# A two-layer mixer kernel: the change of layers overlapped with the last products, and q's and k's rotary products, a tanh and a weight sum moved in time

## The chip, the cores and the metric

The kernel is one program on one core of a Trainium2 chip, written for the engines directly: TensorE (PE, matrix products), VectorE (DVE), ScalarE (ACT), GpSimd (POOL) and SyncE (SP, which here only issues DMAs). Each engine runs its own list of instructions in order; they meet at semaphores. The metric is the device time of one execution in microseconds, the median of several.

## The reference

Each of two layers normalises x (1024 rows of 1024), projects it with one large matrix, runs four token mixers on slices of the projection, gates them, projects again and adds to x. A last norm follows.

```python
for l in range(DEPTH):                     # DEPTH = 2
    h = _rmsnorm(x, norm_g[l])
    p = h @ w_in[l]
    ...                                    # split into pa, pb, pc, pd, dz, pg
    oa = _chunk_band_attention(...) * silu(az)
    ob = _hgrn2(...) * silu(bz)
    oc = _dsa(_rope(q), _rope(k), v, _rope(qi), _rope(ki), cwi) * silu(cz)
    od = _rwkv7(...) * silu(dz)
    y = sum(sigmoid(g) * (o @ w_branch[l, n]))   # over the four mixers
    x = x + y @ w_out[l]
return _rmsnorm(x, final_g)
```

In `_dsa` each query keeps its 256 keys of largest index score.

## The kernel before, in words

All is in float32. The transposed normalised input `hT` (8 tiles of 128 features x 1024 rows) stays in SBUF. The large projections are done by a scheme of seven half-size products in place of eight (`PRODUCTS`): the left sides are sums of quarters of `hT` (`pool_h_sums`), the right sides are sums of quarters of the weights, t1 to t4 (`pool_w_sums`), and both kinds of sums are made by GpSimd. A unit is one block of weights, or two side by side for row-wise results ("rows units": ("C", (2, 3)), ("B", (1, 2)), ("A", (1, 2))), for which a unit has four pairs of row tiles of seven pieces, numbered 0 to 6. ScalarE copies each piece out of its PSUM bank, some into a staging buffer (`rows_stage` or a part of `wr`), from which GpSimd adds it to its place (pieces 1, 4 and 5). There are two banks for this, `G`. For a rows unit the right side t2 is made in halves, and the third piece (number 2) needs the first half.

These pieces are the filling of the whole layer: TensorE makes them in steps (`pe_fill`, two matmul instructions each) wherever the mixers leave room, by constants such as `TOPK_FILL`, the steps beside the top-k search. The order on every engine is written out beforehand. ScalarE copies filled banks at fixed places: `beside(k, half)` says how many steps of TensorE are to be taken as done at search bit k.

The search of mixer C runs over 32 bits, once a layer. In each bit VectorE makes a candidate (line 1493) and compares four row tiles with it (line 1497), ScalarE compares two (line 1411), and VectorE counts. `dve_rope_qk` makes the rotary products of q and k (lines 1448 to 1450, three instructions for each of two parts) at the bits in `qk_bits`. `act_z_gate` makes the tanh of a gate at bit `Z_BIT` = 22 (line 1422).

At the layer's end, `pe_tail` makes the branch products and then the output products, in four pairs of row tiles of seven pieces (line 730). VectorE adds them to x (line 951, `dve_out`), and `act_norm` and `dve_norm` norm each finished row tile for the next layer (lines 891 to 917). Barriers of all engines and a clearing of the semaphores follow. The next layer begins with 64 transposes (`pe_transpose_x`, line 413) and their 16 evacuations of 128x512 (`evac_x`, lines 929 and 931). Then come the products with `wki` (line 1346) and the first pieces. SyncE's list (`sp_loads`, `sp_tail`) is sorted by what each load waits for; the whole of x goes to DRAM in `x_cur` at the start of each layer (line 857) and is read back near the end (line 820). Some waits are on that store, `x_saved`, since it reads the place that is used next. The calls that the diff touches are these:

Of the kernel before, what the change touches and what calls it, by code (L numbers as in the profile page):

```python
# [46 lines left out]
TOPK_FILL = 194  # L47
# [125 lines left out]
def gated_merge_kernel(nc, x, w_in, w_branch, w_out, params, toep, consts, cos_sin, a_mask, final_g, out):  # L173
    ctx = ExitStack()
    with ctx:
# [44 lines left out]
        x_rows = x_cur.rearrange("(i p) d -> p i d", p=P)  # L220

# [32 lines left out]
        for l in range(DEPTH):  # L254
# [70 lines left out]
            def is_rows(u):  # L325
                return len(units[u][1]) == 2
# [76 lines left out]
            def pe_transpose_x(pe):  # L403
                if l == 0:
                    pe.wait_ge(sg("ident_loaded"), 16)
                for half in range(2):
                    if l == 0:
                        pe.wait_ge(sg("rows_normed"), 4 * half + 4)
# [6 lines left out]
                for kt in (KT - 2, KT - 1):  # L415
                    jobs.stored(pe, ("x", kt, 1))

# [158 lines left out]
            def pool_h_sums(pool):  # L576
# [3 lines left out]
                for kt in (KT - 2, KT - 1):  # L580
                    jobs.stored(pool, ("x", kt, 1))
# [11 lines left out]
            def pool_w_sums(pool, u, which):  # L593
# [4 lines left out]
                if 1 in which:  # L598
                    k, b11 = units[u][1][0], right(u, "b11")
                    pool.wait_ge(sg(f"fill_w_loaded{k % 2}"), 16 * (k // 2 + 1))  # L600
                    if is_rows(u):
                        k0, k, halved = half_k // 2, units[u][1][1], 2 * rows_units(u)
# [3 lines left out]
                        pool.wait_ge(sg("w_half_sums"), halved + 1)  # L606
                        pool.wait_ge(sg(f"fill_w_loaded{k % 2}"), 16 * (k // 2 + 1))
                        pool.tensor_tensor(t2[:, 0:k0], b22[:, 0:k0], t1[:, 0:k0], ALU.subtract).then_inc(sg("w_half_sums"), 1)
                    else:
                        pool.tensor_tensor(t1, b12, b11, ALU.subtract).then_inc(sg("w_sums"), 1)  # L610
                if 2 in which:
                    k0 = half_k // 2 if is_rows(u) else 0
                    pool.wait_ge(sg("w_sums"), done + 1)
# [6 lines left out]
            def pool_fills(pool, key=None):  # L620

                upto = len(fills) if key is None else jobs.fills_by[key]
                while pooled[0] < upto:
# [17 lines left out]
                    if p == 4 and last and same:  # L641
                        pool_w_sums(pool, u + 1, (2, 3))
                    if p == 6 and last and more:
# [3 lines left out]
                        else:  # L647
                            pool.wait_ge(sg("pool_added"), adds_before(u + 1))
                            pool_w_sums(pool, u + 1, (1, 2, 3))
# [49 lines left out]

            wbs = [H(at0, 2).rearrange("p (k c) -> p k c", k=2) for at0 in (4, 6, 17, 8)]  # L700
            ths = H(12, 4).rearrange("p (n c) -> p n c", n=8)

            def pe_tail(pe):
# [17 lines left out]
                for i in range(NT // 2):  # L721
                    for p, (y_side, w_side, fresh) in enumerate(PRODUCTS):
# [9 lines left out]
                        jobs.filled(ins, key)  # L732

# [65 lines left out]
            def sp_tail(sp, l):  # L799

                jobs.stored(sp, ("o", ORDER[-1], NT - 1))
                sp.dma_start(wbs[3], w_branch[l:l + 1, BR[ORDER[3]]].rearrange("l (k p) c -> p (l k) c", p=P))\
                  .then_inc(sg("last_wb_loaded"), 16)
                for n, t in enumerate(tail):
# [12 lines left out]
                    if n == 32:  # L817
                        sp.dma_start(xin[:, 0:4, :], x_rows[:, 0:4, :]).then_inc(sg("xr_loaded"), 16)
                jobs.ready(sp, ("branch", len(tail) - 1))
                sp.dma_start(xin[:, 4:8, :], x_rows[:, 4:8, :]).then_inc(sg("xr2_loaded"), 16)  # L820
                if l + 1 < DEPTH:
                    sp.wait_ge(sg("next_par_loaded"), 16)
                else:
# [13 lines left out]

            def sp_loads(sp, l):
# [1606 lines left out]
```

## Time and profile before

| | us |
|---|---|
| median of 3 executions | 2859.62 (2856.38 to 2860.21) |
| the profiled execution's own time | 2858.69 |
| its span, from first to last instruction | 2856.9 |
| TensorE busy | 2770.7 |
| VectorE busy | 1589.2 |
| ScalarE busy | 961.9 |
| GpSimd busy | 844.0 |

A matrix instruction's duration in the profile overlaps the next one's; the starts are further apart or closer than the durations say. "PEclk" is the granted clock of TensorE, where 1.00 is 2.4 GHz and 0.50 is 1.2 GHz.

### The profile page before, as it was taken

Reading aid. Unit: us, or ns where it says so; the run is one execution under the profiler, and the core shown is the slowest. Engines: PE = TensorE matmul, PEld = TensorE weight load, DVE = VectorE, ACT = ScalarE, POOL = GpSimd, SP = SyncE. Lnnn points to the kernel's source line nnn. Section 1 sums busy time; section 2 is a strip of 40 time slices with the busy share of each in tenths; the row PEclk is TensorE's granted clock in tenths of the full one; section 3 lists DMA queues with packets and bytes.
Section 4 is the critical chain, followed back from the end, with each engine's and each line's share of the span. In section 5 each row is a group of like instructions: output and inputs, shape, how many; then the busy total and the mean of one; then the engine's idle time right before and its main releaser. Section 6 shows DMA issues by size and latency. Waiting matters only on the chain. (4 is left out here: it accounts for less than half of the span.)

```text
span 2856.9 us, 45851 instructions
## 1 busy us (share of the span) xinstructions
PE 2770.7 (97%) x18640; PEld 1499.8 (52%) x18640; DVE 1589.2 (56%) x2979; ACT 961.9 (34%) x1820; POOL 844.0 (30%) x578
## 2 busy tenths in 40 slices
PE   7999999999999999999999999999999999999998
PEld 4446444466565566544444464444665745655443
DVE  2689876664506742365228897767544087322743
ACT  3345655311214324500114466643112242245001
POOL 4334322321334332133052333124114342321320
PEclk9999999999999999999999999999999999999999
DMA  5221111101111123083042111112102111221731
GB/s 213 63 59 45 45 49 41 63 32 33 57 30 59 61 83 106 19 276 107 0 159 56 50 54 34 45 41 78 33 18 71 35 44 61 79 104 53 254 99 59
DMA packets 135145, 204.61 MB, mean 72 GB/s; under 512 B 9080, under 2 KB 89112, under 8 KB 134168
## 3 DMA queue, kind: packets, MB, share of 16 engines
q1 hardware_dynamic: 116344, 167.59, 18.5%
q10 hardware_dynamic: 18592, 34.09, 3.2%
q8 instruction: 149, 2.44, 0.4%
q14 instruction: 60, 0.49, 0.1%
HBM read 146.07 MB, written 48.78 MB: 68 GB/s over the span
## 5 line engine op out<-in xcount | busy, mean ns | idle before, releaser
L474 PE MATMUL ps<-hT,wr 128*128 128x512 f32 x1792 | 828.2, 601 | 5.6 <-ACT xo L537 4.3
L474 PEld LDWEIGHTS ps<-hT,wr 128*128 128x128 f32 x1792 | 328.5, 191 | 377.1 <-issue 358.8
L474 PE MATMUL ps<-sums,wr 128*128 128x512 f32 x896 | 426.3, 602 | 1.9 <-ACT xo L537 1.2
L637 POOL TENSOR_TENSOR gts<-gts,wr 128x512 f32<-128x512 f32 x96 | 159.7, 1663 | 688.4 <-ACT wr L528 422.1
L1114 DVE CUSTOM_DVE_ANT_0 arena<-ps,arena 128x640 f32<-128x640 f32 (+7 forms) x128 | 90.3, 705 | 338.4 <-PE ps L1014 324.0
L474 PEld LDWEIGHTS ps<-sums,wr 128*128 128x128 f32 x896 | 161.3, 191 | 177.9 <-issue 164.0
L716 PE MATMUL ps<-xo,arena 128*128 128x512 f32 x512 | 220.2, 592 | 1.6 <-ACT gts L541 1.6
L474 PE MATMUL ps<-wr 128*128 128x512 f32 x448 | 211.7, 602 | 0.0
L528 ACT ACTIVATE wr<-ps 128x512 f32<-128x512 f32 x168 | 99.6, 593 | 316.4 <-PE ps L474 272.3
L1497 DVE TENSOR_SCALAR_CACHE_REDUCE arena<-arena,sm 128x384 f32<-128x384 uint16 (+7 forms) x256 | 192.8, 808 | 2.2
L610 POOL TENSOR_TENSOR wr<-wr 128x512 f32<-128x512 f32 x56 | 79.4, 1417 | 326.9 <-PE ps L474 322.7
L1411 ACT ACTIVATE arena<-arena,sm 128x896 f32<-128x896 uint16 (+3 forms) x128 | 139.4, 1089 | 74.2 <-DVE sm L1493 74.0
L716 PEld LDWEIGHTS ps<-xo,arena 128*128 128x128 f32 x512 | 97.1, 190 | 124.6 <-issue 124.6
L891 ACT ACTIVATE arena<-arena 128x1024 f32<-128x1024 f32 x24 | 25.4, 1059 | 395.5 <-DVEq L970 392.3
L537 ACT ACTIVATE arena<-ps 128x256 f32<-128x256 f32 (+1 forms) x144 | 68.5, 476 | 215.1 <-PE ps L474 123.6
L471 PE MATMUL ps<-wr,hT 128*128 128x256 f32 x576 | 134.2, 383 | 0.0
L1081 ACT ACTIVATE arena<-ps 128x512 f32<-128x512 f32 (+3 forms) x192 | 88.4, 461 | 135.3 <-PE ps L1025 133.8
L637 POOL TENSOR_TENSOR arena<-arena,wr 128x512 f32<-128x512 f32 x48 | 67.9, 1415 | 218.2 <-ACT wr L528 126.5
L547 ACT ACTIVATE gts<-ps 128x512 f32<-128x512 f32 x96 | 57.0, 594 | 222.2 <-PE ps L474 218.9
L474 PEld LDWEIGHTS ps<-wr 128*128 128x128 f32 x448 | 81.4, 191 | 91.0 <-issue 85.9
L618 POOL TENSOR_TENSOR wr<-wr 128x512 f32<-128x512 f32 x56 | 87.8, 1568 | 118.7 <-PE ps L474 118.7
L1470 DVE SCALAR_TENSOR_TENSOR arena<-arena,sm 128x512 f32<-128x512 f32 (+3 forms) x140 | 104.9, 749 | 28.6 <-ACT arena L1393 24.0
(309 smaller groups left out, 4411.7 us busy)
## 6 DMA issues: line engine op xcount, KB each, us to landing
wr<-in_w_in SPq DMA_DIRECT2D x62, 1024.0 KB, 5.3
gate_tanh<-gts ACTq DMA_DIRECT2D x128, 256.0 KB, 2.1
arena<-gate_tanh SPq DMA_DIRECT2D x128, 256.0 KB, 3.0
x_cur<-arena SPq DMA_DIRECT2D x2, 4096.0 KB, 24.8
arena<-in_w_branch SPq DMA_DIRECT2D x8, 1024.0 KB, 8.6
wr<-in_w_out SPq DMA_DIRECT2D x8, 1024.0 KB, 7.5
arena<-x_cur SPq DMA_DIRECT2D x4, 2048.0 KB, 8.3
wr<-in_w_in SPq DMA_DIRECT2D x14, 512.0 KB, 3.7
```

Source lines behind the costliest of these rows:

```text
L471: ins = pe.matmul(ap[:, 0:NCB], lhsT=left(h_side, kt)[:, P * i:P * i + P], rhs=right(u, w_side)[:, kt, :], start=fresh and kt == 0, stop=k ...
L474: ins = pe.matmul(ap, lhsT=right(u, w_side)[:, kt, :], rhs=left(h_side, kt), start=fresh and kt == 0, stop=kt == half_k - 1, skip_group_ch ...
L528: jobs.emptied(act.activation(stage_of(u), src, ACT.Copy), key)
L610: pool.tensor_tensor(t1, b12, b11, ALU.subtract).then_inc(sg("w_sums"), 1)
L618: pool.tensor_tensor(t4, b21, t2, ALU.subtract).then_inc(sg("w_sums"), 1)
L637: pool.tensor_tensor(dst, dst, stage_of(u), ALU.add).then_inc(sg("pool_added"), 1)
L716: ins = pe.matmul(ap, lhsT=wbs[ORDER.index(b)][:, k2, P * ct:P * ct + P], rhs=xo[:, 2 * ORDER.index(b) + k2, 512 * half:512 * half + 512], ...
L1081: ins = act.activation(probs_t[u % 3][:, P * g:P * (g + n)], ap[:, 0:P * n], ACT.Copy)
L1114: ins = dve.tensor_tensor_reduce(out=rows[u % 2][:, 0:P * nb], in0=ap[:, 0:P * nb], in1=bias(i, h, nb), scale=HD ** -0.5, scalar=-3e38, op ...
L1411: act.activation(compared[i], half_keys(k // 16, i), ACT.Sign, bias=cand[:, j:j + 1], scale=-1.0, accum_out=count[:, j:j + 1]).then_inc(sg ...
L1470: ins = dve.scalar_tensor_tensor(acc, r, wgt, acc, ALU.mult, ALU.add)
L1497: ins = dve.tensor_scalar(compared[i], half_keys(part, i), cand[:, j:j + 1], None, ALU.is_lt, ALU.add, accum_out=count[:, j:j + 1])
```

## The change

Between the layers: the transposes for layer 1 are made in layer 0, pair by pair: those of the first pair before the fourth pair's output products, the others after them (`pe_turn_next`), with evacuations of 128x256 by ScalarE and VectorE inside the norm loops (`evac_next`). `wki` of layer 1 is loaded, and six of eight row tiles of x are stored, before the barrier; two are stored first thing in layer 1. Layer 0 stores no x: it reads the input again. At its start the last four row tiles come by two loads and not four. The other parts: `qk_bits` from 4 and 12 to 9 and 14, with the table of `beside` rewritten; the tanh as one half at bit 22 and one at 23; t1 of a rows unit that follows a unit of the other kind is made after piece 4 and not after piece 6; `TOPK_FILL` from 194 to 198. The diff, with the unchanged lines between the edits mostly left out and the indents halved:

```diff
 BETWEEN_FILL = 11
-TOPK_FILL = 194
+TOPK_FILL = 198
...
+x_tiles = x[0].rearrange("(i p) d -> p i d", p=P)
...
   def pe_transpose_x(pe):
-    if l == 0:
-      pe.wait_ge(sg("ident_loaded"), 16)
+    pe.wait_ge(sg("ident_loaded"), 16)
     for half in range(2):
-      if l == 0:
-        pe.wait_ge(sg("rows_normed"), 4 * half + 4)
+      pe.wait_ge(sg("rows_normed"), 4 * half + 4)
...
+  def next_banks(i):
+    if i == 2:
+      return [(bk, (2 * n, 2 * n + 1)) for n, bk in enumerate((T, O, G[0], G[1]))]
+    return [(S2[n], range(4 * n, 4 * n + 4)) for n in range(2)]
+  def pe_turn_next(pe, i):
+    pe.wait_ge(sg("rows_normed"), (NT if l == 0 else 0) + 2 * i + 2)
+    for n, (bk, kts) in enumerate(next_banks(i)):
+      key = ("next", i, n)
+      ap = jobs.open(pe, key, bk)
+      for m, kt in enumerate(kts):
+        for a in range(2):
+          c0 = 256 * m + P * a
+          ins = pe.transpose(ap[:, c0:c0 + P], xo[:, i + 4 * a, P * kt:P * kt + P], ident)
+      jobs.filled(ins, key)
+  def evac_next(eng, odd, pairs):
+    for i in pairs:
+      for n, (bk, kts) in enumerate(next_banks(i)):
+        if n % 2 != odd:
+          continue
+        key = ("next", i, n)
+        ap = jobs.ready(eng, key)
+        for m, kt in enumerate(kts):
+          dst = hT[:, kt, :].rearrange("p (a i c) -> p a i c", a=2, i=4)[:, :, i, :]
+          rows = ap[:, 256 * m:256 * m + 256].rearrange("p (a c) -> p a c", a=2)
+          g = Pr("norm_g", kt, kt + 1)
+          if odd:
+            ins = eng.tensor_scalar(dst, rows, g, None, ALU.mult)
+          else:
+            ins = eng.activation(dst, rows, ACT.Copy, scale=g)
+        jobs.emptied(ins, key)
...
     a21, a22 = hT[:, 0:half_k, 512:], hT[:, half_k:, 512:]
-    for kt in (KT - 2, KT - 1):
-      jobs.stored(pool, ("x", kt, 1))
+    if l == 0:
+      for kt in (KT - 2, KT - 1):
+        jobs.stored(pool, ("x", kt, 1))
...
       if is_rows(u):
-        k0, k, halved = half_k // 2, units[u][1][1], 2 * rows_units(u)
+        k0 = half_k // 2
         pool.tensor_tensor(t1[:, k0:], b12[:, k0:], b11[:, k0:], ALU.subtract).then_inc(sg("w_sums"), 1)
-        pool.wait_ge(sg("w_half_sums"), halved + 1)
-        pool.wait_ge(sg(f"fill_w_loaded{k % 2}"), 16 * (k // 2 + 1))
-        pool.tensor_tensor(t2[:, 0:k0], b22[:, 0:k0], t1[:, 0:k0], ALU.subtract).then_inc(sg("w_half_sums"), 1)
       k0 = half_k // 2 if is_rows(u) else 0
+      if is_rows(u):
+        k = units[u][1][1]
+        pool.wait_ge(sg("w_half_sums"), 2 * rows_units(u) + 1)
+        pool.wait_ge(sg(f"fill_w_loaded{k % 2}"), 16 * (k // 2 + 1))
+        pool.tensor_tensor(t2[:, 0:k0], b22[:, 0:k0], t1[:, 0:k0], ALU.subtract).then_inc(sg("w_half_sums"), 1)
...
         pool_w_sums(pool, u + 1, (2, 3))
+      if p == 4 and last and more and is_rows(u + 1):
+        jobs.ready(pool, key)
+        pool_w_sums(pool, u + 1, (1,))
           pool.wait_ge(sg("pool_added"), adds_before(u + 1))
-          pool_w_sums(pool, u + 1, (1, 2, 3))
+          pool_w_sums(pool, u + 1, (2, 3) if is_rows(u + 1) else (1, 2, 3))
...
+  wki = H(15, 0.5625).rearrange("p (k c) -> p k c", k=KT)
...
         jobs.filled(ins, key)
+      if l + 1 < DEPTH:
+        for turned in {2: (0,), 3: (1, 2, 3)}.get(i, ()):
+          pe_turn_next(pe, turned)
...
+    residual = x_rows if l else x_tiles
...
       if n == 32:
-        sp.dma_start(xin[:, 0:4, :], x_rows[:, 0:4, :]).then_inc(sg("xr_loaded"), 16)
+        sp.dma_start(xin[:, 0:4, :], residual[:, 0:4, :]).then_inc(sg("xr_loaded"), 16)
     jobs.ready(sp, ("branch", len(tail) - 1))
-    sp.dma_start(xin[:, 4:8, :], x_rows[:, 4:8, :]).then_inc(sg("xr2_loaded"), 16)
+    sp.dma_start(xin[:, 4:8, :], residual[:, 4:8, :]).then_inc(sg("xr2_loaded"), 16)
     if l + 1 < DEPTH:
+      sp.wait_ge(sg("y_piece"), len(tail))
+      load_wki(sp, l + 1).then_inc(sg("wki_loaded"), 16)
+      for n, i in enumerate(pair_rows[0:6]):
+        sp.wait_ge(sg("new_rows"), n + 1)
+        sp.dma_start(x_rows[:, i, :], xin[:, i, :]).then_inc(sg("x_saved"), 16)
       sp.wait_ge(sg("next_par_loaded"), 16)
+      sp.wait_ge(sg("wki_loaded"), 16 * 2)
+      sp.wait_ge(sg("x_saved"), 16 * 6)
...
+  def store_last_rows(sp, l):
+    for i in pair_rows[6:8]:
+      sp.dma_start(x_rows[:, i, :], xin[:, i, :]).then_inc(sg("x_saved"), 16)
+  def xin_free(eng):
+    if l:
+      eng.wait_ge(sg("x_saved"), 16 * 2)
+    else:
+      eng.wait_ge(sg("rows_normed"), NT)
+  def load_wki(sp, layer):
+    src = w_in[layer:layer + 1, :, KI0:KI0 + 72].rearrange("l (k p) c -> p (l k) c", p=P)
+    return sp.dma_start(wki, src)
-    loads = [(None, MIX["C"]["sp"])]
+    x_turned = None if l else ("x", KT - 1, 1)
+    loads = [] if l else [(None, MIX["C"]["sp"])]
+    if l:
+      loads.extend([(None, store_last_rows)])
...
         loads.append((("att", 1, NT - 1), MIX[b]["sp"]))
-    loads.append((("x", KT - 1, 1), MIX["A"]["sp_table"]))
-    loads.append((("x", KT - 1, 1), MIX["C"]["sp_cs"]))
+    loads.append((x_turned, MIX["A"]["sp_table"]))
+    loads.append((x_turned, MIX["C"]["sp_cs"]))
     loads.extend(MIX["C"]["sp_turns"]())
-    loads.append((("x", KT - 1, 1), lambda sp, l: sp.dma_start(x_rows, xin).then_inc(sg("x_saved"), 16)))
...
         act.activation(root[:, i - 1:i], msq[:, i - 1:i], ACT.Sqrt).then_inc(sg("root_" + when), 1)
+      if when == "next" and l + 1 < DEPTH and i in (5, NT):
+        act.wait_ge(sg("next_par_loaded"), 16)
+        evac_next(act, 0, (0,) if i == 5 else (1, 2, 3))
...
           dve.tensor_scalar(xo[:, row, :], xin[:, row, :], inv[:, c], None, ALU.mult).then_inc(sg("rows_normed"), 1)
+      if when == "next" and l + 1 < DEPTH and i in (5, NT + 1):
+        dve.wait_ge(sg("next_par_loaded"), 16)
+        evac_next(dve, 1, (0,) if i == 5 else (1, 2, 3))
...
-    wki = H(15, 0.5625).rearrange("p (k c) -> p k c", k=KT)
...
     qk_turned = U(17.25)
-    qk_bits = {4: 0, 12: 1}
+    qk_bits = {9: 0, 14: 1}
     def sp(sp, l):
-      src = w_in[l:l + 1, :, KI0:KI0 + 72].rearrange("l (k p) c -> p (l k) c", p=P)
-      sp.dma_start(wki, src).then_inc(sg("wki_loaded"), 16)
+      load_wki(sp, l).then_inc(sg("wki_loaded"), 16)
     def sp_cs(sp, l):
-      jobs.ready(sp, ("x", KT - 1, 1))
+      if l == 0:
+        jobs.ready(sp, ("x", KT - 1, 1))
...
         if n:
-          sp.wait_ge(sg("x_saved"), 16)
+          xin_free(sp)
...
     def pe(pe):
-      pe.wait_ge(sg("wki_loaded"), 16)
+      if l == 0:
+        pe.wait_ge(sg("wki_loaded"), 16)
...
         jobs.emptied(act.activation(ki[0:72, 0, 512 * half:512 * half + 512], ap[0:72, :], ACT.Copy), ("C", "ki", 0, half))
-      act.wait_ge(sg("x_saved"), 16)
+      xin_free(act)
...
       def beside(k, half):
-        passed = 18 + (426 * k) // 100 + 2 * half + sum(n for bit, n in ((4, 9), (12, 9), (16, 9), (23, 3), (27, 2)) if k >= bit)
+        later = sum(n for bit, n in ((9, 860), (14, 860), (16, 1120), (23, 260), (27, 250)) if k >= bit)
+        passed = 18 + (426 * k + later) // 100 + 2 * half
...
         beside(k, 1)
-        if k == Z_BIT:
-          act_z_gate(act)
+        if k in (Z_BIT, Z_BIT + 1):
+          act_z_gate(act, k - Z_BIT)
-    def act_z_gate(act):
-      unit_done(act, ("C", 2))
-      act.wait_ge(sg("qk_roped"), 4)
-      act.activation(z_tanh, H(6, 2), ACT.Tanh, scale=0.5).then_inc(sg("z_tanh_C"), 1)
+    def act_z_gate(act, half):
+      if half == 0:
+        unit_done(act, ("C", 2))
+        act.wait_ge(sg("qk_roped"), 4)
+      act.activation(H(17.25 + half), H(6 + half), ACT.Tanh, scale=0.5).then_inc(sg("z_tanh_C"), 1)
...
           if bit == Z_BIT + 4:
-            dve.wait_ge(sg("z_tanh_C"), 1)
+            dve.wait_ge(sg("z_tanh_C"), 2)
...
       eng_name[id(pe)] = "pe"
-      pe_transpose_x(pe)
       if l == 0:
+        pe_transpose_x(pe)
...
         act.wait_ge(sg("par_loaded"), 16)
-      evac_x(act, 0)
+        evac_x(act, 0)
...
         def rows_step(i):
-          dve.wait_ge(sg(f"x_in{i}"), 16)
+          dve.wait_ge(sg(f"x_in{i if i < 4 else i - i % 2}"), 16)
         dve.wait_ge(sg("par_loaded"), 16)
-      evac_x(dve, 1)
+        evac_x(dve, 1)
...
       if l == 0:
-        x_tiles = x[0].rearrange("(i p) d -> p i d", p=P)
         sp.dma_start(con[:, 0:P], consts[:, 0:P]).then_inc(sg("ident_loaded"), 16)
-        for i in range(NT):
+        for i in range(4):
           sp.dma_start(xin[:, i, :], x_tiles[:, i, :]).then_inc(sg(f"x_in{i}"), 16)
+        for i in (4, 6):
+          sp.dma_start(xin[:, i:i + 2, :], x_tiles[:, i:i + 2, :]).then_inc(sg(f"x_in{i}"), 16)
```

## Rows read from the trace of the kernel before

**Rows 1.** The page, part 1: busy time of the engines.
```profile
PE 2770.7 (97%) x18640; PEld 1499.8 (52%) x18640; DVE 1589.2 (56%) x2979; ACT 961.9 (34%) x1820; POOL 844.0 (30%) x578
```
**Rows 2.** Waits of TensorE: who, for whom, us in total, times, longest.
```profile
PE ps L471 <- POOL wr L608: 8.5, 4, 3.7
PE ps L474 <- ACT xo L537: 5.5, 3, 2.2
PE ps L471 <- ACT rows_stage L528: 4.2, 5, 1.2
...
PE ps L474 <- ACT arena L661: 1.2, 1, 1.2
```
**Rows 3.** Timeline at ("C", (2, 3)), layer 0: start, duration, instruction, idle before.
```profile
206.99 1.28 POOL L637 TENSOR_TENSOR arena<-arena,wr 128x512 f32<-128x512 f32 x1 [9.68 <-ACT arena L537]
...
208.75 1.23 DVE L1448 TENSOR_TENSOR arena<-arena,xo 128x1024 f32<-128x1024 f32 x1
...
210.50 3.62 PE L471 MATMUL ps<-wr,hT 128*128 128x256 f32 x16
...
215.48 2.24 POOL L608 TENSOR_TENSOR wr<-wr 128x512 f32<-128x512 f32 x1
...
217.87 4.19 PE L471 MATMUL ps<-wr,sums 128*128 128x256 f32 x8 [3.75 <-POOL wr L608]
...
220.93 0.15 DVE L1493 TENSOR_SCALAR sm<-ps 128x6 f32<-128x6 f32 x1
```
**Rows 4.** Window behind it: stretch, length, busy PE, PEld, DVE, ACT, POOL, PEclk.
```profile
217.90:223.40 5.50, 5.43 (x12) 3.90 (x13) 5.43 (x10) 2.28 (x4) 5.50 (x3) 0.50 0.23 51
```
**Rows 5.** Groups of GpSimd at ("B", (1, 2)), layer 0, 795 to 826 us.
```profile
L615 POOL TENSOR_TENSOR wr<-wr 128x1024 f32<-128x1024 f32 x1 | 2.3, 2344 | 0.0
...
L608 POOL TENSOR_TENSOR wr<-wr 128x512 f32<-128x512 f32 x1 | 1.3, 1257 | 0.0
L637 POOL TENSOR_TENSOR xo<-xo,rows_stage 128x256 f32<-128x256 f32 x1 | 0.7, 721 | 0.0
```
**Rows 6.** Timeline around the tanh, layer 0, and its match in layer 1.
```profile
304.95 0.30 PEld L474 LDWEIGHTS ps<-sums,wr 128*128 128x128 f32 x2 [0.78 <-ACT xo L537]
...
309.70 1.28 ACT L1422 ACT_TABLE_LOAD   x1
...
311.00 1.91 ACT L1422 ACTIVATE arena<-arena 128x2048 f32<-128x2048 f32 x1
...
314.47 12.26 PE L474 MATMUL ps<-hT,wr 128*128 128x512 f32 x24 [2.16 <-ACT xo L537]
...
1733.17 10.57 PE L474 MATMUL ps<-hT,wr 128*128 128x512 f32 x24 [2.16 <-ACT xo L537]
```
**Rows 7.** Line 1114 (first in attention) in 300 to 420 us: VectorE's idle time.
```profile
  PE ps L1014: 18.8, 9
```
**Rows 8.** Timeline at the change of layers.
```profile
1431.07 0.75 DVE L917 TENSOR_SCALAR xo<-arena,sm 128x1024 f32<-128x1024 f32 x1
...
1433.05 1.30 PE L413 MATMUL ps<-con,xo 128*128 128x128 f32 x5 [5.13 <-PEq L2393]
...
1443.80 1.48 PE L1346 MATMUL ps<-hT,arena 128*72 128x512 f32 x3 [0.89 <-DVE hT L929]
```
**Rows 9.** Windows there: all engines, then line 413 on TensorE alone.
```profile
1432.00:1438.60 6.60, 5.55 (x27) 5.58 (x28) 1.66 (x3) 2.06 (x3) 0.00 (x0) 0.50 0.73 192
...
1439.00:1442.50 3.50, 3.50 (x34) 1.00 0.40 138
```
**Rows 10.** Timeline: VectorE reading 128x256 and 128x512 from PSUM.
```profile
373.10 0.42 DVE L1136 TENSOR_TENSOR xo<-ps,xo 128x256 f32<-128x256 f32 x1
...
1442.95 0.75 DVE L929 TENSOR_SCALAR hT<-ps,par 128x512 f32<-128x512 f32 x1
```
**Rows 11.** Timeline at the start: VectorE behind the loads of row tiles 4 and 5.
```profile
10.18 0.15 DVE L904 TENSOR_SCALAR sm<-sm 128x1 f32<-128x1 f32 x1 [0.27 <-DMA arena<-in_x]
...
11.46 0.15 DVE L904 TENSOR_SCALAR sm<-sm 128x1 f32<-128x1 f32 x1 [0.28 <-DMA arena<-in_x]
```

## The prediction

> **What bounds the kernel now.** I read the page first: TensorE is busy for 2770.7 of 2856.9 us [rows 1], so nearly all the time is TensorE's own work, and the change can only win what TensorE waits or runs slowly. The executions' median, 2859.62 us, stands 0.93 above the profiled one's own 2858.69, which is 1.8 above its span; the sum is made on 2858.69 and moved by 0.9. Next I read the waits of TensorE. The reader should look there for those whose longest is near a microsecond or over, since they are single events in named places [rows 2]: two of 3.75 inside the 8.5 us on a weight sum of GpSimd (the other two are 0.5), 5.5 us in three pieces on ScalarE's copies (2.16, 2.16, 1.21), and two of 1.2 inside the 4.2 on `rows_stage`. The chain of waits breaks off at the barrier, where 5.13 us more are lost [rows 8]. Then the timeline around each, and the windows for the granted clock, since a wait here is followed by work at 1.2 GHz: in the 5.5 us after the first weight-sum wait the clock is 0.50 [rows 4], after the barrier it is 0.50 for 6.6 us [rows 9]. A wait costs its length and up to half of what follows.
>
> **Q's rotary products in a later bit, and the weight sum moved ahead.** At search bit 4 VectorE makes q's rotary products, six tensor_tensor instructions, from 208.75 to 220.93 [rows 3]. The first took 1.23 us, so six alone are 7.4; they took 12.2, and GpSimd's sum of 128x512 beside them 2.24 [rows 3] against 1.26 at the same kind of unit boundary without them [rows 5]. TensorE starts the unit ("C", (2, 3)) at 210.50, wants the first half of t2 for its third piece, and waits 3.75 us. Afterwards no rotary product stands there, and `t1` is made behind piece 4 of the unit before. GpSimd's queue is then: the add of piece 4 to 208.3 [rows 3], `t1` in two halves of 1.26 to 210.8, the add of piece 5 to 212.1, half of `t2` to 213.3. TensorE wants it two row pieces after its start, 3.5 us, at 214.0: this wait is gone, with 0.7 us to spare. The add of piece 5 is now queued behind `t1`, which itself may wait for a half block of weights; only the buffer `rows_stage` hangs on it. What is late next is the queue's end: the other half of `t2` (1.26), `t3` and `t4` (2.34 each) and an add of 0.72 [rows 5] reach 220.0, while the sixth piece could start at 210.5 + 5 x 1.75 = 219.2 and needs ScalarE's copy behind that add. About 1.0 us of wait is left. Removed per layer: 3.75 and half of 5.5 for the clock, 6.5 together; and 0.5 of `rows_stage` once; left 1.0. Two layers: 13.5 - 2.0 = **11.5 us**. Bounds: 7.5 if the clock falls all the same, 13.5 if nothing is left.
> At ("B", (1, 2)) nothing collides: TensorE waits 0.5 for the sum and 1.2 for `rows_stage`. Two sums, 2.5 us, leave the queue behind the last piece, so both go but for 0.1 a layer: **3.2 us** (0 if the weights land late, to 3.4).
> The moved products are the same six instructions each and the same four DMAs of turned rows; bit 9 is about 18 us after bit 4 and still in ("C", (2, 3)), where GpSimd only has adds of 0.72, and bit 14 ends close to that unit's end, where the next unit's `t2` is wanted after two pieces of 3.4 us and two sums take 4.5 even at 2.24. Both are costed at nothing; rivals 3 and 5 say what they cost if that cover is gone.
>
> **Tanh in two halves.** ScalarE loads a table (1.28) and makes tanh of 128x2048 (1.91) in one go; the copy that empties TensorE's bank comes late and TensorE waits 2.16 at 314.47 [rows 6]; layer 1 has the same and 1.21 more. The 24 instructions behind it take 12.26 us, in layer 1 10.57 [rows 6], so 1.7 goes to the clock. Now 2.16 + 1.7 + 2.16 + 1.21 = 7.2. With one half in each of two bits, the first bit is 0.95 shorter, so 1.2 of 2.16 is left; the new `later` table asks for copies a little later, I take 1.0 a layer and no fall of the clock: **5.2 us**, between 1.9 (only 0.95 a layer) and 7.2. A comparison now stands between the halves; no table load of this trace is at the comparison's line, so none is added.
> `TOPK_FILL` 194 to 198 makes four steps, eight instructions of 0.44 (10.57 for 24), 3.5 us of work earlier; they are missing later: nothing. It hurts only if the search ends before TensorE arrives. TensorE arrives at attention some 6 us earlier (6.5 + 0.5 - 1.0, 2.9 of tanh, less the four steps' 3.5, and the start's 0.7), the search about as much: a rotary block of 7.4 for 12.2, the tanh, and two bits that were late behind it. In attention VectorE already waits 18.8 us for TensorE in nine pieces [rows 7], which is the cover.
>
> **The change of layers.** Before, the last norm ends at 1431.82, the barrier lets TensorE go at 1433.05, 64 transposes and the last evacuations follow, and layer 1's first product starts at 1443.80 [rows 8]: 15.9 us after layer 0's last product ended (1433.05 - 5.13 = 1427.92). After: 16 transposes at 0.11 (3.5 us for some 33 [rows 9]) stand before pair 3's products: 1.7. The other 48 run beside the norms. VectorE then has 12 evacuations of 128x256 behind the last norm. Such a read of PSUM took 0.42, and 0.75 for 128x512 [rows 10] bounds it above; nearest is 0.42, I take 0.47 for the waits between: 5.6 us, to 1437.5 (1436.9 to 1440.8). ScalarE has as many, but starts 1.5 us sooner, and is hidden. The barrier's 1.23 as now: 1438.7, and 1.7: 1440.4, which is 3.3 earlier. But until now the transposes took the slow clock in place of products: all but 1 us of the 6.6 at 0.50 fell on them. After, TensorE idles about 4 us just before the products; I charge 2.0 (0 to 3.3). Net **1.3 us**, from -3.2 (all at the upper bounds) to 3.9.
> The Trainium skill, "TensorE: Matmul & The Clock Gate", section "HAM oscillation — how this bites in real kernels", says that a TensorE left idle goes back to 1.2 GHz and pays again when it resumes. It speaks against this move. By it the whole sum is the 21.9 below, without it 23.9; the trace agrees [rows 4, 9].
> In SyncE's queue six row stores wait for `new_rows` when it has nothing else to do; two stand first in layer 1, ahead of weights whose first use is behind 14 us of `wki` products. Hidden; if the stores were not, a few us.
>
> **The start.** ScalarE waited for the 4096 KB store in layer 0, and TensorE 1.2 behind it [rows 2]; both go. Against it, rows 4 and 5 now land together, and VectorE's wait for row 4 stands ahead of the norm of row 2, so the transposes start one row later, 1.28 us (10.18 to 11.46 [rows 11]). More of them then run at full speed: 0.5 lost (0 to 1.3). Net **0.7 us** (0 to 1.3).
>
> **Sum.** 11.5 + 3.2 + 5.2 + 1.3 + 0.7 = 21.9 us; 2858.69 - 21.9 + 0.9 = 2837.7. I say **2837.5**, by itself 2832 to 2844.
>
> **The rivals.**
> 1. Less: ScalarE's static order of copies holds TensorE. For it, TensorE's weight load at 304.95 already stands 0.78 for ScalarE's copy with the search running evenly [rows 6]. The low ends then hold: 7.5 + 0 + 1.9 + 0 + 0 = 9.4, 2850. Chance 0.12.
> 2. More: no wait is left at the unit and for tanh, and the clock stays up: 13.5 + 3.4 + 7.2 + 3.3 + 1.3 = 28.7, 2831. Chance 0.14.
> 3. Slower: both rotary blocks meet GpSimd's sums in their new bits. The table grants each 8.6 steps of 0.88, 7.6 us, and not 12.2; TensorE idles 4.6 and loses 2.75 to the clock, four times: 29 us, 2867. It decides from 21.9 / 4 = 5.5 us a block. Against it, only the last microsecond of bit 14's block reaches a sum. Chance 0.04.
> 4. Nothing: TensorE waits at attention C for a search that ends late, for all it won: 2857 to 2861. Against it, [rows 7]. Chance 0.05.
> 5. The adds inside the unit stretch bit 9's and bit 14's products: some 1.8 adds of 0.72 meet each block, 1.3 us a block, four blocks, 5.2 us if TensorE idles for all of it: 2843. Against it, adds come only every few us and TensorE has two banks. Chance 0.10. The Trainium skill, "SBUF — State Buffer", section "Who interferes with whom", says that a VectorE instruction with two SBUF inputs and a GpSimd one shut each other out for a whole instruction; that is this rival, and [rows 3] bear it out.
>
> **How the numbers follow.** The forecast keeps 0.55. The range leaves out rivals 3 and 4 and the outer part of 1 and 2: 2827 to 2850. A difference of 0.2%, 5.7 us, is about what can be told from none. Faster: 0.55 + 0.12 + 0.14 + 0.10 = 0.91; same 0.05; slower 0.04.
>
> **What would show it.** After: no wait over 1.5 us behind GpSimd's sums, which take 1.26; the rotary blocks about 7.4 us; tanh as two of 0.95 with one load and waits of about 1 us behind it; 12.5 to 15 us between the layers' products with slow products after them; the first transposes 1.3 us later. The prediction is wrong if the sixth piece waits over 2 us, if a rotary block takes 12, if the clock falls where it did not, or if attention C opens with a wait.

## The result, and the profile after

The changed kernel takes 2836.06 us (median of 4, 2834.21 to 2839.04) against 2858.0 for the kernel before, run beside it (4 runs, 2854.24 to 2860.21): a ratio of 0.9932, with a 95% interval of 0.992 to 0.9944, 16 to 23 us less. The forecast was 2837.5. The profiled execution took 2839.04, with a span of 2837.3, the slowest of its four; so the two traces differ by 19.6 and the medians by 21.9.

In the page, part 1, TensorE's busy time is 8.3 us less than before [rows 1]; the other 11.3 of the 19.6 are time in which it stood still:

```profile
PE 2762.4 (97%) x18640; PEld 1496.1 (53%) x18640; DVE 1583.2 (56%) x2987; ACT 962.3 (34%) x1830; POOL 819.4 (29%) x578
```

The waits of TensorE, with the columns of [rows 2]. Nothing is left behind `pool_w_sums` or behind the tanh, but line 1924 is new:

```profile
PE ps L1924 <- DVEq L2264: 5.9, 2, 3.0
...
PE ps L506 <- ACT rows_stage L563: 5.0, 8, 0.8
PE ps L1421 <- PEq L2471: 3.2, 1, 3.2
```

Where the 19.6 us came from shows best when both traces are cut at the same products. The times are differences of starts in the timelines; "moved" says that eight instructions of 0.43, 3.4 us of work, went from behind attention C to ahead of it (`TOPK_FILL`), and is taken out of the last column.

| stretch of TensorE | before | after | difference without the moved steps |
|---|---|---|---|
| layer 0: start to first product with `wki` | 23.61 | 24.21 | +0.6 |
| to the first product of ("C", (2, 3)) | 186.89 | 185.71 | -1.2 |
| ("C", (2, 3)), layers 0 / 1 | 55.9 / 55.9 | 50.3 / 50.4 | -5.5 / -5.5 |
| from its end to attention C, 0 / 1 | 91.4 / 90.8 | 89.6 / 89.6 | -5.2 / -4.6 |
| attention C to the transposes of mixer D, 0 / 1 | 216.5 / 214.8 | 218.0 / 218.0 | +1.5 / +3.2 |
| those to ("B", (1, 2)), 0 / 1 | 241.2 / 242.8 | 239.1 / 243.4 | +1.3 / +4.0 |
| ("B", (1, 2)), 0 / 1 | 50.6 / 50.7 | 49.0 / 49.1 | -1.6 / -1.5 |
| last product of ("A", (1, 2)) to layer 1's first product | 347.1 | 342.8 | -4.3 |
| layer 1: first product to ("C", (2, 3)) | 185.6 | 187.4 | +1.8 |
| the rest | | | -2.5 |

**The unit ("C", (2, 3)).** The timeline of layer 0, answering to [rows 3]:

```profile
207.53 1.26 POOL L640 TENSOR_TENSOR wr<-wr 128x512 f32<-128x512 f32 x1
...
209.92 3.72 PE L506 MATMUL ps<-wr,hT 128*128 128x256 f32 x16
209.99 1.27 POOL L675 TENSOR_TENSOR arena<-arena,wr 128x512 f32<-128x512 f32 x1
...
211.39 1.27 POOL L650 TENSOR_TENSOR wr<-wr 128x512 f32<-128x512 f32 x1
...
213.48 1.89 PE L506 MATMUL ps<-wr,sums 128*128 128x256 f32 x8
```
```profile
219.76 1.99 PE L506 MATMUL ps<-wr 128*128 128x256 f32 x8 [0.75 <-ACT rows_stage L563]
```

The half of t2 (line 650) is ready at 212.66, 0.8 before the piece that needs it; the sixth piece waits 0.75, a later one 0.43. The two blocks of rotary products stand at 226.33 and 252.74 and take 8.1 and 8.5 us, for the 12.2 and 8.2 of before. The clock stays at 1.00 here.

**The tanh.** ScalarE in layer 0, answering to [rows 6]: one table load, two halves five microseconds apart, a copy ahead of them:

```profile
302.90 0.57 ACT L572 ACTIVATE xo<-ps 128x512 f32<-128x512 f32 x1
303.49 1.28 ACT L1499 ACT_TABLE_LOAD   x1
304.78 1.06 ACT L1499 ACTIVATE arena<-arena 128x1024 f32<-128x1024 f32 x1
...
306.77 0.57 ACT L563 ACTIVATE wr<-ps 128x512 f32<-128x512 f32 x1
...
308.38 1.04 ACT L1499 ACTIVATE arena<-arena 128x1024 f32<-128x1024 f32 x1
```

TensorE's row beside them has no wait at all, and its 24 instructions take 10.46:

```profile
305.11 10.46 PE L509 MATMUL ps<-hT,wr 128*128 128x512 f32 x24
```

**The change of layers**, answering to [rows 8, 9]: the last product of layer 0 ends at 1419.36, the last norm at 1423.43, VectorE's twelve evacuations follow at 0.40 each, and the barrier lets TensorE go 1.2 behind them. Then the window with the granted clock:

```profile
1419.36 3.96 PE L432 MATMUL ps<-con,xo 128*128 128x128 f32 x32
...
1423.35 4.79 DVE L448 TENSOR_SCALAR hT<-ps,par 128x256 f32<-128x256 f32 x12
...
1429.35 3.69 PE L1421 MATMUL ps<-hT,arena 128*72 128x512 f32 x5 [3.20 <-PEq L2471]
```
```profile
1430.20:1433.60 3.40, 3.40 (x5) 0.97 (x4) 0.00 (x0) 0.00 (x0) 3.40 (x1) 0.50 0.99 322
```

Between the layers' products lie 10.0 us for 15.9, and the price is five products at 1.2 GHz, 1.7 us.

**Mixer D, the surprise.** The transposes of mixer D (line 1924) wait for a chain of VectorE. First its last four instructions in the kernel before, then in the changed one, then GpSimd's sums beside the latter, all in layer 0:

```profile
566.13 2.29 DVE L2182 TENSOR_TENSOR xo<-xo,arena 128x2048 f32<-128x2048 f32 x1 [8.01 <-ACT arena L2092]
568.34 0.19 DVE L2183 COPY sm<-arena 128x32 f32<-128x32 f32 x1
568.56 2.29 DVE L2185 TENSOR_TENSOR arena<-arena 128x2048 f32<-128x2048 f32 x1
570.77 3.35 DVE L2186 TENSOR_TENSOR xo<-xo,arena 128x2048 f32<-128x2048 f32 x1
```
```profile
557.09 2.90 DVE L2259 TENSOR_TENSOR xo<-xo,arena 128x2048 f32<-128x2048 f32 x1 [8.01 <-ACT arena L2169]
559.91 1.24 DVE L2260 COPY sm<-arena 128x32 f32<-128x32 f32 x1
561.19 3.30 DVE L2262 TENSOR_TENSOR arena<-arena 128x2048 f32<-128x2048 f32 x1
564.41 3.35 DVE L2263 TENSOR_TENSOR xo<-xo,arena 128x2048 f32<-128x2048 f32 x1
```
```profile
557.80 3.31 POOL L653 TENSOR_TENSOR wr<-wr 128x512 f32<-128x512 f32 x1
561.07 1.26 POOL L675 TENSOR_TENSOR gts<-gts,wr 128x512 f32<-128x512 f32 x1
562.31 3.31 POOL L656 TENSOR_TENSOR wr<-wr 128x512 f32<-128x512 f32 x1
```

The chain's end grew from 8.0 to 10.7 us. TensorE waits 2.95 for 0.79, and 2.1 us later its clock falls:

```profile
567.87 0.65 PE L1924 MATMUL ps<-con,xo 128*128 128x128 f32 x4 [2.95 <-DVEq L2264]
```
```profile
570.00:573.40 3.40, 3.40 (x17) 2.82 (x16) 0.50 (x1) 1.82 (x6) 0.00 (x0) 0.51 0.02 5
```

Layer 1 has the same wait, 2.95 at 1974.71, and the same fall behind it.

### The profile page after: what moved, and what is told of

Its sections match the earlier page's. It is cut to its first block, busy times and chain, and to the rows that moved or that the text cites. A ratio compares the mean times of both kernels' runs of the same rounds, so it can differ in the third digit from the quotient of the medians.

```text
span 2837.3 us, 45877 instructions
## 1 busy us (share of the span) xinstructions
PE 2762.4 (97%) x18640; PEld 1496.1 (53%) x18640; DVE 1583.2 (56%) x2987; ACT 962.3 (34%) x1830; POOL 819.4 (29%) x578
## 4 chain that ended last, share of the span: by engine, by line
PE 42%; DVE 5%; ACT 1%; issue 1%; POOL 1%; DMA 0%; ACTq 0%; DVEq 0%; POOLq 0%
PE ps L509 21%; PE ps L758 4%; PE ps L506 4%; PE ps L772 3%; PE ps L1089 1%; PE ps L1100 1%; PE ps L1445 1%; PE ps L1113 1%; DVE arena L1832 1%; PE ps L1950 1%; DVE arena L1574 1%; PE ps L1421 1%; PE ps L2012 1%; PE ps L478 0%; PE ps L1942 0%
## 5 line engine op out<-in xcount | busy, mean ns | idle before, releaser
L509 PE MATMUL ps<-sums,wr 128*128 128x512 f32 x896 | 420.5, 598 | 1.4 <-issue 0.7
L675 POOL TENSOR_TENSOR gts<-gts,wr 128x512 f32<-128x512 f32 x96 | 152.8, 1592 | 665.4 <-ACT wr L563 466.6
```

The source lines that it names most:

```text
L509: ins = pe.matmul(ap, lhsT=right(u, w_side)[:, kt, :], rhs=left(h_side, kt), start=fresh and kt == 0, stop=kt == half_k - 1, skip_group_ch ...
L675: pool.tensor_tensor(dst, dst, stage_of(u), ALU.add).then_inc(sg("pool_added"), 1)
```

## The experiments

Times are medians; a kernel without another base is an edit of the changed kernel, 2836.06.

**1. Which step moved the collision in mixer D.**

```diff
-TOPK_FILL = 198
+TOPK_FILL = 194
```

> The changed kernel with TOPK_FILL at 194 again, so that four of TensorE's filling steps stand behind the search and not beside it. Why: the changed kernel waits 2.95 us in mixer D, once a layer, for VectorE's chain (before: 0.79), and the clock is 0.50 for 3.4 us behind it. Between the bonus products and the end of the chain VectorE needed 31.8 us before and 34.2 after; GpSimd's sums stand elsewhere against it. Theory: the four steps moved the pieces, and so GpSimd's sums, against the chain. Then the chain is back at about 32, the wait at 0.8, and the kernel gains 2.16 and up to 1.7 a layer, some 4 to 8 us in all, if nothing is lost at attention C. Rival 1: the chain is stretched by something else, the wait stays at 2.95 and the time at 2836. Rival 2: the search bounds the start of attention C; TensorE then waits up to 3.5 us there in each layer, and the time is 2836 or up to 3 more.

Measured 2828.08 (2826.37 to 2831.17), 0.9897 of before (0.9882 to 0.9912): 8.0 less than the changed kernel. The wait is 0.79 in both layers, with no fall of the clock behind it, and no wait of 3.5 came at attention C (the longest there is 0.78):

```profile
559.81 0.66 PE L1924 MATMUL ps<-con,xo 128*128 128x128 f32 x4 [0.79 <-DVEq L2264]
```

The chain as a whole took 29.1 us (530.6 to 559.7), less than the 31.8 of before: behind the bonus products the clock had fallen there and had not here, and ScalarE's exponentials in the chain stand behind TensorE's steps. Its last four instructions took 8.0. Both rivals fall. The two traces differ by 12.7 us, more than the medians: 4.3 are the waits, 3.4 the clock behind them, and 5.1 are falls behind the bonus products, where the clock fell for 6.8 us in both layers of the changed kernel's trace and here for 3.4 in layer 1 alone. These falls vary among all the kernels (last section), and that they hang on the four steps isn't shown.

The same from the other side, on the kernel before:

```diff
-TOPK_FILL = 194
+TOPK_FILL = 198
```

> The kernel before with TOPK_FILL at 198, nothing else. Theory: the four steps alone shift the pieces against VectorE's chain in mixer D; the wait there goes from 0.79 to about 2.95 in both layers, with the clock down for 3.4 us behind it: 4 us more a layer, less what the steps may cover beside the search, 2860 to 2866. Rival: the wait needs another part of the change too; it stays at 0.79 and the time at 2857.7.

Measured 2862.56 against 2856.2, ratio 1.0025 (1.0016 to 1.0035): 4.6 to 10 us more. The chain's tail is the slow one, instruction for instruction, and so is the wait:

```profile
570.43 2.90 DVE L2182 TENSOR_TENSOR xo<-xo,arena 128x2048 f32<-128x2048 f32 x1 [8.01 <-ACT arena L2092]
573.25 1.24 DVE L2183 COPY sm<-arena 128x32 f32<-128x32 f32 x1
...
581.21 0.66 PE L1847 MATMUL ps<-con,xo 128*128 128x128 f32 x4 [2.95 <-DVEq L2187]
```

So the four steps are the cause by themselves.

**2. Cover the wait, or shorten the chain.**

```diff
-pe_fill(pe, D_FILL["decay"])
+pe_fill(pe, D_FILL["decay"] + (3 if n == 2 else 0))
```

> The changed kernel with three more filling steps (2.6 us of TensorE's work) directly ahead of the products that wait in mixer D; they are missing further behind. Everything ahead of them is as it was, so the chain of VectorE still takes 34.2 us. Theory: the wait is only a lack of cover: 2.95 becomes about 0.4, the clock stays up, 2.6 + 1.7 a layer are won, about 2828. Rival: the mixer's next steps are bound by VectorE too, the wait comes back further on, and the time stays at 2836.

Measured 2835.9. The wait is down to 0.37 and the clock does not fall behind it, and still the next common product of layer 0, in ("B", (1, 2)), starts at 816.31 for 816.33. In layer 1 the stretch from mixer D's transposes to ("B", (1, 2)) does get shorter, 240.4 for 243.4, so the theory held there in part; the medians, 2835.9 and 2836.06, don't show it. For layer 0 it is the rival's result, but not its reason: the waits for VectorE did not grow. TensorE now stands with nothing to wait for that the profile shows, 4.2 us in all in this stretch for 1.0, by the waits of TensorE. The longest, 2.35, came while a load of 1024 KB filled the DMA engines, and the clock fell behind it:

```profile
617.01 0.45 PE L1950 MATMUL ps<-arena 64*64 64x64 f32 x7 [2.35 <-issue]
```
```profile
610.00:614.00 4.00, 3.27 (x166) 2.99 (x160) 2.90 (x5) 0.41 (x1) 1.28 (x1) 1.00 0.77 225
614.00:617.00 3.00, 0.66 (x23) 0.57 (x18) 0.36 (x1) 0.00 (x0) 0.00 (x0) 1.00 0.17 55
```

Instructions come by DMA too, on a queue of their own in the page. That they were late behind the load is argued from these rows, not shown; nothing was run that moves the load alone.

```diff
-pe_fill(pe, D_FILL["decay"])
+pe_fill(pe, (D_FILL["decay"], D_FILL["decay"] - 4, D_FILL["decay"] + 4)[n])
```

> The changed kernel with the mark that lets ScalarE make the second and third exponential of mixer D after 18 of the filling steps and not after 22 (the number of steps ahead of the waiting products stays 33). VectorE waits 8.0 us for the second one in the changed kernel. Theory: the chain ends about 3.4 to 6 us sooner, the wait of 2.95 is gone, and so is the fall of the clock: 2.95 + 1.7 a layer, about 2827. Rival: ScalarE's copies, now queued behind 3.8 us of exponentials, make TensorE wait for its banks, 1 to 2 us a layer, and the time is 2830 or more; or GpSimd's sums meet the chain in its new place and take the gain back.

Measured 2835.24. The chain of layer 0 ends 7.3 us sooner, at 560.4 (1.7 of it is a shorter fall of the clock behind the bonus products), and TensorE's first transposes do not wait. The second four do, for ScalarE, which stands behind an add of GpSimd that is itself late among slowed sums:

```profile
554.89 3.38 POOL L675 TENSOR_TENSOR gts<-gts,wr 128x512 f32<-128x512 f32 x1 [4.11 <-ACT gts L582]
...
564.92 0.63 ACT L594 ACTIVATE gts<-gts 128x512 f32<-128x512 f32 x1 [1.12 <-POOL gts L675]
```
```profile
566.28 0.72 PE L1924 MATMUL ps<-con,xo 128*128 128x128 f32 x4 [2.67 <-ACT arena L2176]
```

The time is the rival's, and of its two reasons the second: GpSimd's sums met the chain in its new place. Its add, 1.26 alone, took 3.38 and then 1.71, and ScalarE stood idle behind it; the exponentials were long done, at 554.3.

**3. The change of layers and the start alone:** `TOPK_FILL` 194, rotary products at 4 and 12 with the old table, the tanh whole, t1 behind piece 6 (the edits of experiments 4 and 5 together).

```diff
-TOPK_FILL = 198
+TOPK_FILL = 194
...
-qk_bits = {9: 0, 14: 1}
+qk_bits = {4: 0, 12: 1}
...
-pool_w_sums(pool, u + 1, (2, 3) if is_rows(u + 1) else (1, 2, 3))
+pool_w_sums(pool, u + 1, (1, 2, 3))
...
-if k in (Z_BIT, Z_BIT + 1):
+if k == Z_BIT:
```

> Only the change of layers and of the start: the changed kernel with TOPK_FILL 194, q's and k's rotary products at bits 4 and 12 with the old table, the tanh in one piece and t1 behind piece 6. Theory, from the changed kernel's trace: the first product of layer 1 comes 4.3 us nearer and 1.7 of it goes to the clock; the wait for the store of x (1.25) is gone, the start costs 0.6; in all 3.3 less than before, 2854.7. The waits of 3.75 and 2.16 are all back, and mixer D waits 0.8 and not 2.95. Rival: mixer D's wait of 2.95 comes with the change of layers; then it is there, and the time is 2858 or more.

Measured 2852.53 against 2857.71, ratio 0.9985 (0.9976 to 0.9994): 1.7 to 6.9 us less. The waits of 3.75 and 2.16 are back, mixer D waits 0.79, and the stretch that ends at layer 1's first product is 342.8 long, as in the changed kernel. The theory holds; it missed a second wait on GpSimd in the unit, 1.01 and 0.73, which before did not have.

**4. The unit ("C", (2, 3)): rotary products or t1?**

```diff
-if p == 4 and last and more and is_rows(u + 1):
-  jobs.ready(pool, key)
-  pool_w_sums(pool, u + 1, (1,))
...
-pool_w_sums(pool, u + 1, (2, 3) if is_rows(u + 1) else (1, 2, 3))
+pool_w_sums(pool, u + 1, (1, 2, 3))
```

> The changed kernel with t1 of a rows unit made behind piece 6 again; the rotary products stay at bits 9 and 14. Theory: the waits of 3.75 us came from VectorE's rotary products beside GpSimd's sums, not from where t1 stood. Then ('C', (2, 3)) waits about 0.5 for the half of t2 and 1.2 for rows_stage, as ('B', (1, 2)) did before: some 1 us more than now in each of the four places, 2840, and the clock does not fall. Rival: t1's place was the cause; then 3.75 and the slow clock behind it are back in each layer and the time is 2849.

Measured 2847.69 (2845.71 to 2849.32). The 3.75 did not come back, and the clock did not fall there. But the half of t2 came 1.6 late, not 0.5, as the add of piece 5 and its wait stand ahead of t1:

```profile
215.87 2.27 PE L506 MATMUL ps<-wr,sums 128*128 128x256 f32 x8 [1.60 <-POOL wr L650]
...
222.80 1.99 PE L506 MATMUL ps<-wr 128*128 128x256 f32 x8 [1.22 <-ACT rows_stage L563]
```

The unit takes 52.7 and not 50.3, ("B", (1, 2)) 50.6 and not 49.0, which makes 8 of the 11.6 us; the rest lies in other places of the trace, among them a longer fall of the clock behind the barrier and one more in layer 1.

```diff
-qk_bits = {9: 0, 14: 1}
+qk_bits = {4: 0, 12: 1}
...
-later = sum(n for bit, n in ((9, 860), (14, 860), (16, 1120), (23, 260), (27, 250)) if k >= bit)
-passed = 18 + (426 * k + later) // 100 + 2 * half
+passed = 18 + (426 * k) // 100 + 2 * half + sum(n for bit, n in ((4, 9), (12, 9), (16, 9), (23, 3), (27, 2)) if k >= bit)
```

> The changed kernel with q's and k's rotary products at bits 4 and 12 again and the old table of copies; t1 stays behind piece 4. Theory: the sums of GpSimd that stand beside the rotary products take 2.24 and not 1.26, the half of t2 comes about 2 us late, a second wait of about 1 follows, and the clock falls: 4 to 6 us a layer, 2845 to 2848. Rival: with t1 ahead the queue has room enough, and the rotary products may stand at bit 4: 2836 to 2838.

Measured 2856.47, ratio 0.9999 of before: 20 us, far more than either theory gave. The unit is 55.9 long, as before: t1 ahead alone is worth nothing, for the sums still take 2.24 beside the rotary products. (This run has the old table too; by experiment 5 its numbers make the unit shorter, not longer.) The lengths of the unit for neither, t1 alone, rotary alone and both are 55.9, 55.9, 52.7 and 50.3, from the first product to the last. And waits of 1.30 and 1.22 stand at the tanh, though it is made in halves: the stretch from there to attention is 93.4 long for 89.6. The unit and this stretch, in two layers, make 18.7 of the 20 us.

**5. The tanh: halves or table?**

```diff
-if k in (Z_BIT, Z_BIT + 1):
-  act_z_gate(act, k - Z_BIT)
+if k == Z_BIT:
+  act_z_gate(act)
```

> The changed kernel with the tanh in one instruction of 128x2048 at bit 22; the new table of copies stays. Theory: the copy behind it comes late and TensorE waits about 2.16 once a layer, with the clock at 0.50 for 3.4 us behind it in one layer at least: 2.2 to 3.9 a layer, 2840 to 2844. Rival: the table was what mattered and the halves are worth nothing: 2836.

Measured 2835.48. No wait stands at the tanh, though ScalarE makes it in one instruction of 1.91:

```profile
302.85 0.58 ACT L572 ACTIVATE xo<-ps 128x512 f32<-128x512 f32 x1
303.44 1.28 ACT L1498 ACT_TABLE_LOAD   x1
304.74 1.91 ACT L1498 ACTIVATE arena<-arena 128x2048 f32<-128x2048 f32 x1
```

The theory falls, the rival stands. So the table was undone, with the halves and the bits kept (in the expectation the direction is told wrong: fewer steps taken as done put a copy later):

```diff
-((9, 860), (14, 860), (16, 1120), (23, 260), (27, 250))
+((9, 900), (14, 900), (16, 900), (23, 300), (27, 200))
```

> The changed kernel (TOPK_FILL 198, tanh in halves, rotary products at 9 and 14) with the steps of the old table at the new bits: 9, 9, 9, 3, 2 in place of 8.6, 8.6, 11.2, 2.6, 2.5. At the tanh ScalarE then takes 1.4 steps fewer as done than now, so it copies earlier and less. Theory: the new numbers are what freed the tanh; the waits of about 1.3 and 1.2 that stand there with the old table and the old bits come back, and the stretch from the end of ('C', (2, 3)) to attention grows from 89.6 to 92 or 93 us: 2841. Rival: the later rotary products did it; the stretch stays at 89.6 and the time at 2836.

Measured 2844.47. The stretch to attention is 93.4 long for 89.6, in both layers, and the waits are there:

```profile
298.47 3.70 PE L509 MATMUL ps<-sums,wr 128*128 128x512 f32 x8
302.12 3.70 PE L509 MATMUL ps<-wr 128*128 128x512 f32 x8
307.13 1.12 PE L509 MATMUL ps<-hT,wr 128*128 128x512 f32 x2 [1.31 <-ACT xo L572]
```
```profile
301.50 0.57 ACT L563 ACTIVATE wr<-ps 128x512 f32<-128x512 f32 x1
```

Ahead of the tanh the pieces start 3.65 apart, where the changed kernel has 3.43; in the kernel before it was 3.65 too:

```profile
301.30 3.70 PE L474 MATMUL ps<-hT,wr 128*128 128x512 f32 x8
304.95 3.70 PE L474 MATMUL ps<-sums,wr 128*128 128x512 f32 x8
```

The rows of this run show why: a piece ended at 298.5 and was copied at 301.5, 3.0 later, so TensorE ran at the pace of a search bit, 3.65. With the new numbers a copy comes a half bit earlier, 1.0 behind its piece's end, and the tanh with its table load fits into the slack. The new numbers have a price: with the old ones the unit ("C", (2, 3)) is 49.5 long for 50.3, as its wait of 0.43 is gone. In these two stretches the new table is thus worth 3.0 us a layer, 5.9 of the 8.4 between the medians; the rest lies in falls of the clock elsewhere.

**6. The clock behind the barrier, and the start**, both with `TOPK_FILL` 194 (2828.08).

```diff
+if i == 3:
+  jobs.stored(pe, ("next", 2, 0))
+  for _ in range(28):
+    pe.transpose(T.ap[:, 0:P], ident, ident)
```

> The changed kernel with TOPK_FILL 194 (2828.1 by itself) and 28 idle transposes of the identity behind the last transposes of the change of layers, so that TensorE works for about 3 us of the 3.2 that it waits at the barrier; they make nothing that is used. Theory: the clock falls behind the barrier because TensorE stood idle; with the transposes it stays up, the products with wki take 13.3 and not 15.0, and 1.7 us are won: 2826.4. Rival: the clock falls all the same, or the transposes hold TensorE past the barrier: 2828 to 2829.

Measured 2831.35 (2830.42 to 2833.82). The clock stays up, and the products up to ("C", (2, 3)) take 185.7 for 187.1:

```profile
1428.19 2.34 PE L1425 MATMUL ps<-hT,arena 128*72 128x512 f32 x5 [1.19 <-PEq L2475]
```
```profile
1428.20:1431.60 3.40, 3.40 (x8) 1.16 (x9) 0.00 (x0) 0.00 (x0) 3.40 (x1) 1.00 0.82 287
```

But TensorE came to the barrier 1.05 us late with it. That idling was the cause of the fall is shown: in the ten traces with a wait of 3.2 us there the clock fell each time, for 3.4 or 6.8 us, and in the two with the gap filled (this one and the last below) it did not. That filling it pays is not shown: in layer 0 the clock fell for 6.8 us behind the bonus products of mixer D instead, where the kernel with 194 alone had no fall, and in layer 1 the stretch from mixer D's transposes to ("B", (1, 2)) took 246.0 for 243.1, with 4.9 us of `issue` waits at 64x64 products there for 2.6.

```diff
-for i in range(4):
+for i in range(NT):
   sp.dma_start(xin[:, i, :], x_tiles[:, i, :]).then_inc(sg(f"x_in{i}"), 16)
-for i in (4, 6):
-  sp.dma_start(xin[:, i:i + 2, :], x_tiles[:, i:i + 2, :]).then_inc(sg(f"x_in{i}"), 16)
```

> The changed kernel with TOPK_FILL 194 and the rows of x loaded by eight DMAs again. Theory: the norm of row tile 2 no longer waits for the pair of tiles 4 and 5; the first transposes start near 12.7 and not 14.0, the first product near 23.6 and not 24.3: 0.6 to 0.9 us less, 2827.4. Rival: the first product depends on the last rows alone and stays where it is, 2828.

Measured 2827.88. The first transposes start at 12.57 for 14.19 and the first product at 23.02 for 24.46, 1.4 less, but the medians don't tell it from nothing. Last, the three together, with 16 idle transposes:

```diff
-TOPK_FILL = 198
+TOPK_FILL = 194
...
+  for _ in range(16):
+    pe.transpose(T.ap[:, 0:P], ident, ident)
...
-for i in range(4):
+for i in range(NT):
```

> The changed kernel with TOPK_FILL 194, the rows of x by eight DMAs, and 16 idle transposes (not 28) in the gap at the change of layers, so that they end before VectorE's last evacuation. Theory, by the traces of the three kernels that had one of these each: 2828.1, less 1.4 at the start, less up to 1.7 for the clock behind the barrier without the 1.05 that 28 transposes held it: 2825 to 2826. Rival: the clock falls at other places instead (behind the bonus products of mixer D, before the attentions), as its falls moved from run to run so far, and the median stays at 2828.

Measured 2829.68 (2827.29 to 2832.06): the rival. No fall stands behind the barrier, one of 6.8 us stands at 528.2 behind the bonus products, and the stretch to ("B", (1, 2)) in layer 1 is 245.6 long, as with 28 transposes. Why it grows in these two isn't shown. No kernel here is clearly faster than the changed one with `TOPK_FILL` at 194, which is 8 us faster than the changed kernel.

## Why the prediction was right, and where it was not

The total was right, 2837.5 for 2836.06, but with luck: 10.0 us lost in mixer D, forecast as nothing, were made up by 4.6 more at the tanh, 1.2 more at the change of layers and 2.5 of chance. By its own terms, on the profiled traces:

| term | predicted | measured |
|---|---|---|
| rotary products and t1 at ("C", (2, 3)) | 11.5 | 11.0 |
| ("B", (1, 2)) | 3.2 | 3.2 |
| tanh | 5.2 | 9.8, most of it by the table |
| change of layers | 1.3 | 2.5 |
| start | 0.7 | 0.6 |
| `TOPK_FILL`, mixer D | 0 | -10.0 |
| chance (an `issue` wait of 1.67 and slow clock in layer 1 before) | | 2.5 |

- **The unit.** GpSimd's queue ran as worked out: t2's half was forecast at 213.3 and came at 212.7, TensorE was to want it at 214.0 and did at 213.5. What is left, 0.75 and 0.43, is the 1.0 charged. Experiment 4 adds that neither half of the change does it alone.
- **("B", (1, 2)).** The sum is right; the 0.58 still waited there stands behind weights that landed late: t1 waited 1.87 for a load, the bound named in the prediction.
- **Tanh.** The step that failed is "the new `later` table asks for copies a little later": that holds for bits 9 to 15, by 0.4 and 0.8 steps; from bit 16 on it asks for them earlier, by 1.4 steps at the tanh. By experiment 5 that is 7.6 of the 9.8 us (less 1.8 that it costs in the unit). The halves, on which the term was built, are worth nothing beside it. The term also left out that TensorE ran at the pace of the search ahead of the tanh, 3.65 a piece for 3.43.
- **`TOPK_FILL`.** The step that failed is "they are missing later: nothing". The steps add no work, but every piece that follows stands eight instructions elsewhere against VectorE's chain, and with it GpSimd's sums. Of the 10.0, 4.3 are the waits, 3.4 the clock behind them, 1.7 a longer fall in layer 1 than before, about 1.9 waits on nothing shown there, less 1.3 for a wait in attention C that went. It is rival 5's mechanism, in a place that the prediction did not look at. One of its own signs of being wrong came true here: the clock fell where it had not, behind both waits. The Trainium skill, "SBUF — State Buffer", section "Who interferes with whom", says that a VectorE instruction with two inputs in SBUF contends with a GpSimd one that reads SBUF, and calls the shared ports an exclusive lock: the trace agrees, with GpSimd's 1.26 become 3.31 beside a VectorE instruction of 2.3. A VectorE copy of 0.19 became 1.24 beside a sum too.
- **The change of layers.** 12 evacuations took 4.8, not 5.6; the barrier 1.2; the clock 1.7 for the 2.0 charged. The "12.5 to 15 us between the layers' products" was a slip: 15.9 less 3.3 less the 1.7 of transposes that moved ahead is 10.9, and 10.0 was measured. The Trainium skill, "TensorE: Matmul & The Clock Gate", section "HAM oscillation — how this bites in real kernels", holds that an idle TensorE pays when it resumes; with the gap filled it did not pay (experiment 6), so the trace agrees on the cause.
- **The start.** The transposes came 1.29 later, as forecast, at 13.91 for 12.62.
- **The rivals.** 3 and 4 are out: no block of rotary products took over 8.5, and attention C opened without a wait. Rival 1's time is out, but its mechanism was at work in the kernel before: ScalarE's order of copies set the pace of 3.65, and the new table lifted it. Rival 2 was right for the search and wrong as a whole. Rival 5 was right that the moved blocks stretch, to 8.1 and 8.5 for the 7.4 reckoned, and wrong that TensorE idles for it: the only wait beside them is the 0.43.

## What to carry to other kernels

Work that is "only moved" along a static schedule shifts the phase of everything behind it: list which two engines share a resource there and look at both their rows, in every later stage, before costing the move at nothing. Where one engine empties another's banks by a table, look at how long a finished piece waits for its copy, and try the table before shortening the instruction in the way. Undo each part alone: here two parts worth 0 and 3.1 us a layer by themselves made 5.5 together, one part was worth nothing, and one cost 8.

## What the runs showed of the hardware

- A wait on "issue" of TensorE, 2.35 us, beside a load of 1024 KB at 0.77 of the DMA engines, in a stretch of 64x64 products; the kernels before and after show such waits of 0.7 to 1.7 in mixers D and B. Their cause is open.
- At or just behind the 32 narrow bonus products of mixer D (128x2, 3.63 us in the traces where the clock stays up beside them) the clock fell for 6.8 us, for 3.4 or not at all: 12, 8 and 8 times in the two layers of the fourteen traces, which costs 3.4, 1.7 or 0 us. Differences of this size between two traces prove nothing.
- At the change of layers the clock fell for 3.4 us in five traces and for 6.8 in five, behind one and the same wait of 3.2 us; behind waits of 1.19 and 1.46 it did not.
